# Attention with queries on the partitions: row maximum, the denominator from the exponential's accumulated sum, probabilities turned by transposing DMAs

## What is computed

```python
def sink_attention(q, k, v, sinks, mask):
    # q (..., Tq, Hkv, G, hd); k, v (..., Tk, Hkv, hd); sinks (Hkv, G)
    s = jnp.einsum('...qhgd,...khd->...hgqk', q, k).astype(jnp.float32) * (HEAD_DIM ** -0.5)
    if mask is not None:
        s = jnp.where(mask, s, NEG_INF)
    sk = sinks.astype(jnp.float32)[:, :, None, None]          # (Hkv, G, 1, 1)
    m = jnp.maximum(jnp.max(s, axis=-1, keepdims=True), sk)
    p = jnp.exp(s - m)
    denom = jnp.sum(p, axis=-1, keepdims=True) + jnp.exp(sk - m)
    p = (p / denom).astype(v.dtype)
    return jnp.einsum('...hgqk,...khd->...qhgd', p, v)
```

## Time and profile before

| | us |
|---|---|
| median of 3 runs | 4405.48 |
| lowest, highest | 4329.9, 4933.42 |
| the profiled execution | 4362.66 |
| its span on the slowest core (core 5) | 4361.1 |
| spans of the cores | 4324.5 to 4361.1 |
| PE busy | 4138.1 (95%) |
| DVE, ACT, POOL busy | 2138.7, 1800.3, 1017.5 |

### The profile page before, as it was taken

One profiled execution on the slowest core, in us unless ns is written; L12 is line 12 of the kernel. 1 busy time (PEld: TensorE's weight loads), 2 busy tenths in 40 slices (PEclk: granted clock), 3 DMA queues, 4 the chain that ended last, 5 costly groups with the idle time before them and its releaser, 6 DMA issues.

```text
span 4361.1 us, 62941 instructions; the slowest of 8 cores (4324.5 to 4361.1 us)
## 1 busy us (share of the span) xinstructions
PE 4138.1 (95%) x20672; PEld 1846.3 (42%) x20672; DVE 2138.7 (49%) x3136; ACT 1800.3 (41%) x3523; POOL 1017.5 (23%) x1087
## 2 busy tenths in 40 slices
PE   6799798898999999999999999999999999999998
PEld 2344343343444444444444444444444444444444
DVE  3655364454564445455454545545454554545432
ACT  5554253353443525344252534435253433525322
POOL 0000000000002233332323323232332333233232
PEclk9899899999999999999999999999999999999999
DMA  9486887776447354553636454363545536364422
GB/s 187 75 160 115 189 175 151 196 176 186 145 136 226 132 192 146 188 157 130 213 124 200 142 181 157 130 212 124 200 145 180 164 131 212 114 200 148 161 97 94
DMA packets 200671, 696.95 MB, mean 160 GB/s; under 512 B 106017, under 2 KB 106594, under 8 KB 130722
## 3 DMA queue, kind: packets, MB, share of 16 engines
q1 hardware_dynamic: 72194, 506.31, 33.8%
q0 software_dynamic: 28144, 146.55, 16.8%
q10 hardware_dynamic: 100016, 40.06, 4.6%
HBM read 699.88 MB, written 69.99 MB: 177 GB/s over the span
## 4 chain that ended last, share of the span: by engine, by line
PE 81%; DVE 7%; DMA 4%; issue 3%; ACT 3%; POOL 1%; DVEq 0%; ACTq 0%; SPq 0%; POOLq 0%
PE ps L310 81%; DMA yp<-tmpf 2%; DVE tmpf L338 1%; DMA big<-hst 1%; ACT junk L317 1%; ACT L315 1%; DVE stt L690 1%; DVE hst L338 1%; DMA ring<-wfo 1%; DVE gvf L338 1%; DVE gvn L338 1%; DVE dent L622 1%; POOL stt L327 1%; DVE tmpf L327 1%; PE ps L473 0%
## 5 line engine op out<-in xcount | busy, mean ns | idle before, releaser
L310 PE MATMUL ps<-big,ring 128*128 128x512 bf16 x12032 | 2711.6, 384 | 60.2 <-DVE tmpf L338 46.3
L310 PEld LDWEIGHTS ps<-big,ring 128*128 128x128 bf16 x12032 | 1156.9, 99 | 1512.9 <-issue 244.2
L310 PE MATMUL ps<-ring,big 128*128 128x512 bf16 (+1 forms) x5376 | 1165.7, 375 | 46.0 <-POOL big L327 16.3
L310 PEld LDWEIGHTS ps<-ring,big 128*128 128x128 bf16 x5376 | 524.0, 99 | 628.7 <-issue 110.0
L327 POOL TENSOR_TENSOR big<-tmpf 128x512 bf16<-128x512 f32 x360 | 476.2, 1323 | 1048.8 <-ACT tmpf L322 812.0
L315 ACT ACTIVATE big<-ps 128x512 bf16<-128x512 f32 (+1 forms) x552 | 339.1, 626 | 603.8 <-PE ps L310 447.1
L315 ACT ACTIVATE y<-ps 64x512 bf16<-64x512 f32 (+2 forms) x1024 | 488.5, 478 | 53.3 <-PE ps L310 0.6
L338 DVE SCALAR_TENSOR_TENSOR tmpf<-tmpf,ps 128x512 f32<-128x512 f32 x352 | 240.8, 684 | 518.9 <-ACT tmpf L315 518.9
L622 DVE RECIPROCAL dent<-dent 128x256 f32<-128x256 f32 (+1 forms) x264 | 442.7, 1694 | 6.4
L338 DVE SCALAR_TENSOR_TENSOR tmpf<-big,ps 128x512 f32<-128x512 bf16 x256 | 174.9, 686 | 488.0 <-PE ps L310 478.9
L317 ACT ACTIVATE junk<-ps 128x512 bf16<-128x512 f32 x260 | 155.1, 597 | 599.5 <-PE ps L310 522.4
(11 more groups left out here) (101 smaller groups left out, 1881.6 us busy)
## 6 DMA issues: line engine op xcount, KB each, us to landing
ring<-s_wfi SPq DMA_DIRECT2D x148, 1024.0 KB, 5.5
ring<-s_win SPq DMA_DIRECT2D x138, 1024.0 KB, 6.8
ring<-s_wfo SPq DMA_DIRECT2D x54, 1024.0 KB, 5.9
ring<-w_in POOLq DMA_DIRECT2D x38, 1024.0 KB, 12.5
ring<-s_wap SPq DMA_DIRECT2D x29, 1024.0 KB, 9.6
ring<-wfi POOLq DMA_DIRECT2D x28, 1024.0 KB, 10.7
ring<-s_wout SPq DMA_DIRECT2D x27, 1024.0 KB, 5.4
ring<-s_wgp SPq DMA_DIRECT2D x25, 1024.0 KB, 11.2
```

What stands on the lines that cost most here:

```text
L310: m.op(PE, lambda e: e.matmul(out, lhsT=lhsT, rhs=rhs, start=start, stop=stop), reads=reads, writes=[("ps", b)])
```

## The change

The prompt attention puts queries on the partitions. `attn_S` issues 16 matmuls for a pair, each with 64 rows and 64 columns of the array and 192 key columns, into banks 0 to 3; DVE takes the row maximum of each bank (`TENSOR_REDUCE`, 4 for a pair) and forms the negated, scaled maximum with the sink. `attn_exp` runs 8 exponentials of 128x192 with the maximum as bias and the sum accumulated on the way, and one of the sinks (128x8). `attn_norm` adds, takes an 8-column reciprocal and multiplies the probabilities (three 128x512 operations on PX). `attn_T` turns 12 blocks of 128x128: by one DMA that ACT issues where PX is POOL (88 pairs), by 12 PE transposes into banks 0 and 1 and two ACT copies where PX is DVE (40 pairs). `attn_PV` issues 12 matmuls of 64 rows, 64 columns and 256 columns of data into bank 4 (`BO`), and `attn_fin` is a copy. The ones-matmuls, the large reciprocals and the zeroed corners go. `Vt` becomes `V2`, in which each 64-frame chunk of values stands on both partition halves, filled by four 64x128 casts for a block in place of one 128x256. The sample attention follows the same scheme. Small constants share buffers with others, and `junk` is the third of the three probability buffers `Pb`.

```diff
@@ -244,15 +245,22 @@
         kT = sb("kT", [128, 2, 640], BF16)
-        Vt = sb("Vt", [128, 5, 256], BF16)
+        V2 = sb("V2", [128, 10, 128], BF16)
...
-        PT = y0[:].bitcast(BF16).rearrange("p a (c n) -> p (a c) n", c=2)
-        dent = sb("dent", [128, 2, 512], F32)
+        y0v = y0[:].bitcast(BF16).rearrange("p a n -> p (a n)")
+        PTt = [y0v[:, 1536 * i:1536 * (i + 1)].rearrange("p (a n) -> p a n", n=128) for i in range(2)]
...
+        NP = 3
+        Pb = sb("Pb", [128, NP, 1536], BF16)
+        junk = Pb[:, 2, 0:1024]
...
+        sat = sb("sat", [128, NP, 6, 8], F32)
...
@@ -509,160 +524,223 @@
...
+                            for c in range(2):
+                                for e in range(2):
+                                    tcopy(DVE, V2[64 * e:64 * e + 64, 2 + 2 * b + c, :],
+                                          banks[b_][64 * c:64 * c + 64, 256 + 128 * e:384 + 128 * e], [("ps", b_)],
+                                          [("V2", 2 + 2 * b + c)])
...
+        BO = 4
+        MX, NM, SK, EK, DEN, RC = range(6)
...
+        def parts(t, b):
+            if t["first"] and b == 0:
+                return [(slice(0, 64), 2), (slice(64, 128), 1)]
+            return [(slice(0, 128), 0)]
+
+        def finish_max(t, n, ns, w):
+            m.op(DVE, lambda e: e.scalar_tensor_tensor(out=sa(n, NM, cols=w), in0=sa(n, MX, cols=w), scalar=-0.125,
+                                                       in1=ns[0], op0=ALU.mult, op1=ALU.min),
+                 reads=sk_(n, MX) + ["snk"], writes=sk_(n, NM))
+            tt(DVE, sa(n, SK, cols=w), ns[1], sa(n, NM, cols=w), ALU.add, sk_(n, NM) + ["snk"], sk_(n, SK))
+
+        def attn_S(t, n, b, tp):
...
+            pr = parts(t, b)
+            for g in range(4):
+                for c in range(2):
+                    p0 = pr[c][1] if len(pr) == 2 else 0
+                    for e in range(2):
+                        es_ = slice(64 * e, 64 * e + 64)
+                        bk = 2 * e + g // 2
+                        o0 = 192 * (g % 2) + 64 * p0
+                        k0 = 128 * b + 64 * c + 64 * p0
+                        w = 192 - 64 * p0
+                        mm(bk, banks[bk][64 * c:64 * c + 64, o0:o0 + w],
+                           t["big"][es_, C_Q + 4 * tp + g, b * 128 + 64 * c:b * 128 + 64 * c + 64],
+                           kT[es_, tp, k0:k0 + w], True, True,
+                           [("kT", sl, tp) for sl in (b, b + 1)] + BK(t, C_Q + 4 * tp + g, C_Q + 4 * tp + g + 1, (b,)))
+            for gp in range(2):
+                for e in range(2):
+                    bk = 2 * e + gp
+                    for rows, p0 in pr:
+                        iv = banks[bk][rows, 0:384].rearrange("p (g k) -> p g k", g=2)[:, :, 64 * p0:192]
+                        ov = sa(n, MX, rows, slice(4 * gp + e, 4 * gp + e + 3, 2))
+                        m.op(DVE, (lambda iv, ov: lambda e: e.tensor_reduce(out=ov, in_=iv, axis=AX.X, op=ALU.max))(
+                            iv, ov), reads=[("ps", bk)], writes=sk_(n, MX))
+            finish_max(t, n, (snk[:, 0, tp, :], snk[:, 1, tp, :]), slice(0, 8))
+
+        def attn_exp(t, n, b, tp):
...
+            Pv = Pb[:, n % NP, :].rearrange("p (a h k) -> p a h k", a=3, h=8)
+            if len(pr) == 2:
+                memset(DVE, Pv[:, 0, :, :], 0.0, [("P", n % NP)])
+                memset(DVE, Pv[0:64, 1, :, :], 0.0, [("P", n % NP)])
+            for g in range(4):
+                for e in range(2):
+                    bk = 2 * e + g // 2
+                    h = 2 * g + e
+                    for rows, p0 in pr:
+                        iv = banks[bk][rows, 192 * (g % 2) + 64 * p0:192 * (g % 2) + 192]
+                        ov = Pv[rows, p0:3, h, :]
+                        iv = iv.rearrange("p (a k) -> p a k", k=64)
+                        m.op(ACT, (lambda iv, ov, rows, h: lambda e: e.activation(
+                            out=ov, in_=iv, func=AF.Exp, bias=sa(n, NM, rows, slice(h, h + 1)), scale=0.125,
+                            accum_out=sa(n, DEN, rows, slice(h, h + 1))))(iv, ov, rows, h),
+                            reads=[("ps", bk)] + sk_(n, NM), writes=[("P", n % NP)] + sk_(n, DEN))
+            act(sa(n, EK), sa(n, SK), AF.Exp, sk_(n, SK), sk_(n, EK))
+
+        def attn_norm(t, n):
+            w = slice(0, 1) if t["sample"] else slice(0, 8)
+            tt(DVE, sa(n, DEN, cols=w), sa(n, DEN, cols=w), sa(n, EK, cols=w), ALU.add, sk_(n, DEN, EK), sk_(n, DEN))
+            m.op(DVE, lambda e: e.reciprocal(out=sa(n, RC, cols=w), in_=sa(n, DEN, cols=w)), reads=sk_(n, DEN),
+                 writes=sk_(n, RC))
...
+            Pv = Pb[:, n % NP, :].rearrange("p (a h k) -> p a h k", a=3, h=8)
+            for a in range(3):
+                tt(PX[0], Pv[:, a, :, :], Pv[:, a, :, :], sa(n, RC).unsqueeze(2).to_broadcast([128, 8, 64]), ALU.mult,
+                   sk_(n, RC) + [("P", n % NP)], [("P", n % NP)])
...
+            if PX[0] == POOL:
+                m.dma(ACT, ("pt", n % 2), pt[:, :, :], pv, reads=[("P", n % NP)], writes=pt_keys(n), transpose=True)
+                return
+            for bk, k0, k1 in ((0, 0, 8), (1, 8, 12)):
+                bv = banks[bk][:].bitcast(BF16)
+                for k in range(k0, k1):
+                    m.op(PE, (lambda bv, k, k0: lambda e: e.transpose(out=bv[:, (k - k0) * 128:(k - k0 + 1) * 128],
+                                                                      in_=pv[:, k * 128:(k + 1) * 128],
+                                                                      identity=ident[:]))(bv, k, k0),
+                         reads=[("P", n % NP), "ident"], writes=[("ps", bk)])
+                act(pt[:, k0:k1, :], bv[:, 0:(k1 - k0) * 128].rearrange("p (k t) -> p k t", t=128), AF.Copy,
+                    [("ps", bk)], pt_keys(n))
 
         def attn_PV(t, n, b, tp):
...
+            for c in range(2):
+                p0 = 2 - c if first else 0
+                for p in range(p0, 3):
+                    for e in range(2):
+                        es_ = slice(64 * e, 64 * e + 64)
+                        ov = banks[BO][es_, :].rearrange("p (g q) -> p g q", g=4)[:, :, 64 * c:64 * c + 64]
+                        mm(BO, ov, V2[es_, 2 * b + c + p, 64 * tp:64 * tp + 64],
+                           pt[es_, 4 * p:4 * p + 4, 64 * c:64 * c + 64], p == p0, p == 2,
+                           [("V2", 2 * b + c + p)] + pt_keys(n))
...
+            tcopy(DVE, a_out, banks[BO][:, 0:W].rearrange("p (g q) -> p g q", g=4), [("ps", BO)],
+                  BK(t, C_Q + 4 * tp, C_Q + 4 * tp + 4, (bl,)))
...
         def plan_attn(t, t0, span):
             pairs = [(b, tp) for b in range(2 if t["sample"] else 4) for tp in range(2)]
-            W = span / (len(pairs) + 1)
-            for n in range(len(pairs) + 1):
+            W = span / (len(pairs) + 1.6)
+            for n, (b, tp) in enumerate(pairs):
                 a = t0 + n * W
-                if n < len(pairs):
-                    b, tp = pairs[n]
-                    ev(a, (lambda n, b, tp: lambda: attn_S(t, n, b, tp, 1))(n, b, tp))
-                    ev(a + 0.5 * W, (lambda n, b, tp: lambda: attn_S(t, n, b, tp, 2))(n, b, tp))
-                if n > 0:
-                    b, tp = pairs[n - 1]
-                    k = n - 1
-                    ev(a + 0.1 * W, (lambda n, b, tp: lambda: attn_PV(t, n, b, tp))(k, b, tp))
-                    ev(a + 0.3 * W, (lambda n: lambda: attn_recip(t, n, 0))(k))
-                    ev(a + 0.5 * W + 0.01, (lambda n: lambda: attn_recip(t, n, 1))(k))
-                    ev(a + 0.75 * W, (lambda n, b, tp: lambda: attn_fin(t, n, b, tp))(k, b, tp))
+                f = lambda fn, *x: lambda: fn(*x)
+                ev(a, f(attn_S, t, n, b, tp))
+                ev(a + 0.25 * W, f(attn_exp, t, n, b, tp))
+                ev(a + 0.8 * W, f(attn_norm, t, n))
+                ev(a + 1.5 * W, f(attn_T, t, n))
+                ev(a + 2.3 * W, f(attn_PV, t, n, b, tp))
+                ev(a + 2.45 * W, f(attn_fin, t, n, b, tp))
...
-        def zero_corners(pp, eng):
-            Pv = PT[:, pp, :].rearrange("p (g q) -> p g q", g=4)
-            ap = Pv[0:64, :, 64:128] if pp % 2 == 0 else Pv[64:128, :, 0:64]
-            memset(eng, ap, 0.0, [("PT", pp)])
```

287 lines of the change are left out of this document (130 added, 157 removed).

## The result

The changed kernel takes 4945.89 us in the median against 4376.93 for the kernel before, measured side by side: **1.137 times the time, with a 95% interval of 1.123 to 1.151**. The prediction said slower, and 4520 us; the direction holds, the size does not. The profiled execution has a span of 4908.3 us on core 7, against 4361.1. In some executions of every kernel here the cores of one die, or of both, show a lower granted clock and take some per cent longer; figures are from the others unless a lower clock is named.

The account below looks back on a forecast made before the run. PE was taken as the bound, never waiting in the FFN stage. Late pairs +65, early pairs +67, tile 0 +9 and casts +15 us gave +156 on 4362.66: 4520 us, range 4350 to 4660.

Parts of the forecast that it names:

- PE visits: PE's score and PV matmuls of a pair: 1.36 us in place of 1.92, -72 us over 128 pairs.
- transposes: Twelve PE transposes where PX is DVE: 0.66 us for each of 40 pairs, +26 us.
- late waits: In 88 pairs with PX on POOL, PE waits 1.0 us for a unit's bank and 0.3 for the transposing DMA.
- early waits: In 32 early pairs, the second transposes wait for the seventh exponential of the pair between: mean 2.0 us a pair.
- tile 0: The 8 pairs of the first tile, with other units around them: about +1.1 us each, 9 us.
- casts: Four 64x128 value casts for one delay the first scores: about 1 us for each of 15 tiles, 15 us.
- the window: One pair's period in an FFN stage, 10.3 us long, followed from its scores through units U1 to U5.
- rival of the queueing quarters: Small score and PV matmuls run one after another, 1.6 us more a pair: 4652 us, chance 0.16.
- The exponentials start at 3.35: ScalarE's block starts 3.35 us after the scores begin if U0 is an odd unit, 4.5 if even.
- at nothing: GpSimd's three multiplications a pair, 3.5 us, cost nothing, since a unit's product can come 3.5 us late.
- 0.48 apiece: Each 128x192 exponential on ScalarE with accumulated sum takes 0.48 us, 3.85 for eight.
- the block fits: Rival: exponentials don't wait for one another's sum and follow at 0.27 us or less; 4351 us, chance 0.22.

Follow-up runs that it names:

- best3: Changed kernel with four plain exponentials, no maxima, VectorE sums, moved dates, split multiplications, small bias loaded first, half the value casts on ACT; 1.006 times the kernel before.
- psum_sink: Changed kernel with the sink values read from unused columns of PSUM bank 3 instead of SBUF; span 1.127 times the kernel before, late stages 108.7 us.
- exp_late: Changed kernel with the exponentials due 0.5 of a window behind the scores in place of 0.25; span 1.155 times the kernel before, late stages 122.8 us.
- no_norm: Changed kernel without the multiplication of the probabilities by the reciprocal; PE idles 22.5 us in place of 34.3 in an early stage.
- best: Changed kernel with four plain exponentials, no maxima, VectorE sums, and moved dates for exponentials, multiplications, turning and PV; span 1.017 times the kernel before.
- nm_free: Changed kernel without row maxima and without waits among the eight exponentials, sums still accumulated; 1.037 times the kernel before.
- gap: Kernel before, with a PE wait for two GpSimd operations behind each late pair's second scores; span 1.14 times the kernel before, late stages 144.1 us.

## Why the prediction missed

By its own steps, us for the whole:

| step | predicted | measured |
|---|---|---|
| PE visits, -0.56 a pair | -72 | -0.48 to -0.54 a pair (best3: 83.9 long for 87.7, 83.1 busy for 87.4) |
| transposes, 0.66 a pair | +26 | 0.57 (88.5 - 83.9, a stage of 8) |
| late waits, 1.3 a pair | 114 | 2.64 a pair, 11 x 21.1 = 232: units' banks 1.33 (predicted 1.0), DMA 0.67 (0.3), scores' banks 0.47 (nothing), the rest 0.2 |
| early waits, 2.0 a pair | 64 | 4.1 a pair: 4 x 33.0 = 132 |
| tile 0 | 9 | 63, with the rest of the opening |
| casts | 15 | 14.6 of wait, part of the two rows of waits |
| clock | none | 11 x 4.3 + 4 x 13.3 = 100 |
| broken runs of matmuls | none | 11 x 2.5 + 4 x 2.4 = 37 |

The steps that failed are these: the late waits (118 us short), where the window left out the scores' banks and began the exponentials too early; no term for the clock (100 short), which stood nowhere in the sum; the early waits (68 short), where VectorE's multiplications were priced nowhere; and the opening (54 short).

- **PE's time of a pair was right** to 0.1 us, from the rows of two halves of the array. The rival of the queueing quarters is refuted: a PV visit takes 0.78 and not 1.48. The rule of the Trainium skill (TensorEngine Tiling (Array Packing), Gotcha 1) would have cost PV 0.64 more; the twelve matmuls that write bank 4 from both row halves don't show it.
- **"The exponentials start at 3.35" (or 4.5) failed**: in the late rounds they start 6.0 us behind the start of the scores in the median. I let VectorE begin the maxima at once or one multiplication late, 0.6 us in the mean; it is 1.6. And from the maxima to the first exponential I took 0.3 us; it is 1.23, because GpSimd's multiplications run just then and stretch the one 8-column operation between. That I costed GpSimd "at nothing" looked only at when its result is wanted, not at what it takes away meanwhile. Taking the stretch away (psum_sink) gave 2.5 us a stage back. The Trainium skill (VectorE: DVE Perf Modes, Two Vector instructions with no wait between them) names a second read interface, shared with GpSimd, for the second of two SBUF inputs; the trace agrees, with 0.97 us where both are in SBUF and 0.16 where one is in PSUM.
- **"0.48 apiece" failed**: it is 0.60. The line through two lengths gave 0.32 us for an operation that takes 0.42, and the wait on the neighbour costs 0.21 where 0.08 was taken. That "the successor waits" for the read was a misreading: in the earlier trace rows the successor starts at 2566.51 and the read ends at 2566.61.
- **The window had no second pair in it.** I followed one unit's bank, and that wait was right in kind and nearly in size (1.33 a pair for 1.0). But the scores' four banks have no second copy either, and on them lie 0.5 + 5.4 + 4.6 = 10.5 us against a window of 4.58 units of 1.73 and 1.36 for the visits, 9.3. The wait that this causes by itself is 3.7 us of a late stage; exp_late shows how it grows, to 15.9, when the exponentials come later. How much of the units' waits would be there if the exponentials came on time is not shown: with four exponentials and no maxima they are gone.
- **Early rounds**: the mechanism (transposes wait for exponentials of the pair in between) was right, the size was not: the multiplications of the pair before, 2.29 us on VectorE, stand ahead of the maxima. The text priced them nowhere; without them (no_norm) 11.8 of the 34.3 us of idle time go.
- **The DMA**: 70.4 / 88 = 0.8 us a pair on core 7, 0.67 in the mean of the cores, where 0.3 was taken, within its bounds of 0 to 4.2. Landing is 4.0 us in the median. In `best` the later date of PV and the earlier one of turning remove it. (The rival "the block fits" left out this term's 26 us in its 4351.)
- **The clock** was not in the sum: 100 of 547 us come from it, and 37 from broken runs of matmuls. In this case a us of waiting on PE cost 1.3 to 1.6 us in all.
- **The opening**: eight pairs with few units around them pay their latency in full, the first two with 16 exponentials of 64 rows each (8.2 us). Removing the maxima and the waits (nm_free) takes it from 336 to 308, four exponentials take it to 300. How the rest splits was not settled.

The range (4350 to 4660) had no case in which several terms are wrong at once, and none for the two terms that were missing. The direction was right for the reasons given, the waits and the transposes, and not by luck.

## What to carry to other kernels

Before costing a step by its engine, write down for each buffer that has no second copy the whole loop from one writer to the next, and compare it with the period. Here a us less in the exponentials' block, inside that loop, gave back 0.9 to 1.1 us, while the waits for the turned probabilities went by dates alone, with nothing made cheaper. Then look at what else runs on each engine at that moment, and at waits between neighbours that touch different columns of one buffer: a finer key was worth 10 us a stage. And a wait on PE costs more than its length: give the clock a term of its own.

## What the runs showed of the hardware

- A VectorE operation of 8 columns with two SBUF operands that starts beside a GpSimd operation ends with it (195 of 197 cases): 0.97 and 1.12 us in the median, where it meets the start of one, in place of 0.17. With one operand in PSUM it takes 0.16 to 0.17 beside GpSimd too (psum_sink).
- Exponentials with a sum read follow one another at 0.39 us without a wait between them and at 0.60 with one (128x192); plain ones with the wait at 0.51.
- Sixteen 64x64-tile matmuls of 192 columns pass in 0.46 us, twelve of 256 in 0.78.
- 42.5 us of PE holes in a stage of 87.7 lower the granted clock from 1.00 to 0.87 and lengthen the same matmuls by 14 us (gap). In the changed kernel a break in a run of matmuls adds about 0.15 us to PE's busy time besides (an estimate from 17 more waits and 2.5 us in a late stage).
